# Sample rows in column halves, even column groups, another tile order, and inputs fetched a stage ahead, in a whole decoder layer on one core

## The reference

```
h = rmsnorm(x) * (1 + sc1) + sh1                 # sc, sh, gt from silu(c) @ ada_w
q, k, v, qi, ki, wi, hq, hf, hi, hg = split(h @ w_in)     # 3656 columns
score = sum_h wi[h] * relu(qi[h] . ki)           # 8 index heads x 64
keep the 256 best admissible keys of each query
a = rmsnorm(softmax(q . k over the kept keys) @ v)        # 8 heads, 4 kv heads, x 64
r = gated linear recurrence(hq, hf, hi) per head of 128   # state 128 x 128, 4 heads
r = rmsnorm(r) * silu(hg)
x = x + gt1 * (concat(a, r) @ w_out)
h = rmsnorm(x) * (1 + sc2) + sh2
x = x + gt2 * moe(h)                             # top 1 of 4 groups, top 2 of its 4 experts
y = rmsnorm(x) * (1 + scf) + shf
```

## Time and profile before

| | us |
|---|---|
| median of 3 runs | 1861.36 (1853.93 to 1866.20) |
| the profiled execution, its own time | 1853.43 |
| its span, first to last instruction | 1851.7 |
| TensorE busy | 1618.0 (87%) |
| VectorE busy | 840.5 (45%) |
| ScalarE busy | 388.0 (21%) |
| GpSimd busy | 205.6 (11%) |

### The profile page before, as it was taken

How to read it: one execution, slowest core, us unless ns; L and a number is a source line. 1 busy time by engine, 2 the same in 40 slices (tenths; PEclk the granted TensorE clock), 3 DMA queues, 4 the chain that set the end, 5 groups by cost and what they waited for, 6 DMA issues and landing times. The chain is left out here.

```text
span 1851.7 us, 20887 instructions
## 1 busy us (share of the span) xinstructions
PE 1618.0 (87%) x7594; PEld 784.4 (42%) x7595; DVE 840.5 (45%) x1935; ACT 388.0 (21%) x780; POOL 205.6 (11%) x176
## 2 busy tenths in 40 slices
PE   5998899999999979989996996961799999999970
PEld 3553334444443357765443752641233333333320
DVE  3123469999999135543215452756111111111116
ACT  4003442321111145432224341210000000000002
POOL 0001001100000000010022330100111111111112
PEclk9999999999999989999998798985899999999985
DMA  9112113332333240016447035624899999999924
GB/s 337 47 47 80 46 46 115 119 122 76 122 127 123 81 164 1 1 59 263 183 186 251 13 129 163 213 97 160 311 336 357 367 347 346 348 350 324 326 71 193
DMA packets 133098, 326.21 MB, mean 176 GB/s; under 512 B 16497, under 2 KB 23945, under 8 KB 130442
## 3 DMA queue, kind: packets, MB, share of 16 engines
q1 hardware_dynamic: 116826, 241.95, 37.1%
q0 software_dynamic: 16176, 82.98, 13.5%
HBM read 281.93 MB, written 42.97 MB: 175 GB/s over the span
## 5 line engine op out<-in xcount | busy, mean ns | idle before, releaser
L2639 PE MATMUL banks<-arena 128*64 x1008 | 438.6, 595 | 5.4 <-issue 2.6
L2640 PE MATMUL banks<-arena 128*64 128x512 f32 x1008 | 438.7, 595 | 0.0
L1175 PE MATMUL banks<-arena 128*128 128x512 f32 (+2 forms) x960 | 384.3, 557 | 0.3 <-ACT arena L1308 0.3
L1175 PEld LDWEIGHTS banks<-arena 128*128 128x128 f32 (+1 forms) x960 | 167.4, 188 | 220.7 <-issue 215.1
L2639 PEld LDWEIGHTS banks<-arena 128*64 128x64 f32 x1008 | 136.6, 137 | 282.2 <-issue 282.2
L1459 DVE TENSOR_SCALAR_CACHE_REDUCE arena<-arena 128x384 uint8<-128x384 f32 (+3 forms) x224 | 246.0, 1142 | 3.4
L2640 PEld LDWEIGHTS banks<-arena 128*64 128x64 f32 x1008 | 136.7, 137 | 0.0
L2708 DVE TENSOR_TENSOR arena<-arena,banks 128x256 f32<-128x256 f32 x42 | 15.8, 418 | 262.8 <-PE banks L2640 262.8
L2690 ACT ACTIVATE arena<-banks 128x512 f32<-128x512 f32 x21 | 12.5, 597 | 465.7 <-PE banks L2640 465.7
L1726 DVE CUSTOM_DVE_ANT_0 arena<-banks,arena 128x512 f32<-128x512 f32 (+3 forms) x96 | 51.4, 575 | 76.9 <-PE banks L1662 76.9
L2719 DVE SCALAR_TENSOR_TENSOR arena<-banks,arena 128x1024 f32<-128x1024 f32 x21 | 27.0, 1284 | 129.5 <-PE banks L2640 129.5
(11 more groups left out here) (415 smaller groups left out, 1986.0 us busy)
## 6 DMA issues: line engine op xcount, KB each, us to landing
arena<-in_w SPq DMA_DIRECT2D x63, 2048.0 KB, 13.0
arena<-in_ada_w SPq DMA_DIRECT2D x12, 2048.0 KB, 9.1
arena<-in_w_in SPq DMA_DIRECT2D x7, 2048.0 KB, 7.8
arena<-in_ada_final_w SPq DMA_DIRECT2D x4, 2048.0 KB, 8.1
arena<-in_x_prompt SPq DMA_DIRECT2D x4, 1024.0 KB, 8.2
tmp_hf<-arena SPq DMA_DIRECT2D x16, 256.0 KB, 2.0
tmp_hq<-arena SPq DMA_DIRECT2D x16, 256.0 KB, 2.0
arena<-in_x_prompt SPq DMA_DIRECT2D x8, 512.0 KB
```

The lines of the kernel that those rows point to most:

```text
L1175: ins = pe.matmul(ps[0:m, ring[n] % 2, 0:cols], lhs(a), rhs(a), start=(a == 0), stop=(a == KD - 1))
L2639: pe.matmul(ps[0:HP, bank, :], x[:, 0:HP], Wt[:, bass.ds(at, 1), off:off + width].rearrange("p o a -> p (o a)"), **kw)
L2640: return pe.matmul(ps[HP:P, bank, :], x[:, HP:P], Wt[:, u, off:off + width], **kw)
```

## The change

Five things change. (1) In `front` each product of the 64 sample rows is issued as two of 256 columns, whose results go to the lower and the upper 64 partitions of a bank; ScalarE copies two halves. (2) The feature chunks' column groups are 363, 363 and 362 wide. (3) `prompt_attention` takes tile 7 first and tile 0 last: `tile(n)` stands wherever n // 4 or i named a tile, and i only counts. (4) In `hgrn` the first eight partial rows have a place each in R, and the transposed attention goes to buffers that the norms use later; `scaled` waits for the stores instead. (5) The modulation rows, norm gains, router weights and x of tiles 0 and 1 are loaded in `hgrn`, behind SyncE's waits for the end of certain parts, into places that have come free; some buffers of `project_out` move.

```diff
+O_GT, O_SH, O_XR, O_G2 = O_HQ, O_S0, O_S0 + 2 * D, O_HF
+O_WR = O_G2 + D
...
+def next_inputs(k):
+    ar = k.ar
+    gt, sc, sh = ar.view(O_GT, 2, D), ar.view(O_GT + 2 * D, 2, D), ar.view(O_SH, 2, D)
+    return gt, sc, sh, ar.view(O_G2, D), [ar.view(O_XR + b * D, D) for b in range(2)], ar.view(O_WR, KD, NR)
...
@@ hgrn @@
     def turned_to(i):
-        return (R[:, i % 2, :] if i < NPRE else V[:, 4 + i % 2, :]).rearrange("p (a n) -> p a n", n=P)
+        return ((sq, sqa)[i % 2] if i < NPRE else V[:, 4 + i % 2, :]).rearrange("p (a n) -> p a n", n=P)
     def staged(n):
-        return R[:, 4 + n % 4, :] if n < 2 * NPRE else V[:, n % 4, :]
+        return R[:, 1 + n, :] if n < 2 * NPRE else V[:, n % 4, :]
...
@@ hgrn, sync @@
+            gt, sc, sh, g2, x, wr = next_inputs(k)
+            moves = scale_shift_parts(k, (g2, t["norm2_g"]), [(gt, 2), (sc, 4), (sh, 3)])
+            sp.wait_ge(s["att"], NQ)
+            sp.dma_start(*moves[6]).then_inc(k.s_next["mod"], 16)
+            sp.dma_start(wr[:, :, 0:4], t["w_group"].rearrange("o (a p) n -> p (o a) n", p=P)).then_inc(k.s_next["wr"], 16)
+            sp.dma_start(wr[:, :, 4:NR], t["w_expert_router"].rearrange("o (a p) n -> p (o a) n", p=P)).then_inc(k.s_next["wr"], 16)
             sp.wait_ge(s["sa"], 2 * GH)
-            sp.dma_start(t["hgrn_sample"].rearrange("o s h p e -> p (o s) h e"), S0.rearrange("p s (h e) -> p s h e", e=DK)).then_inc(s["out"], 16)
+            sp.dma_start(t["hgrn_sample"].rearrange("o s h p e -> p (o s) h e"), S0.rearrange("p s (h e) -> p s h e", e=DK)).then_inc(k.s_next["s0"], 16)
+            sp.wait_ge(s["o"], NQ)
+            for move in moves[0:4]:
+                sp.dma_start(*move).then_inc(k.s_next["mod"], 16)
+            sp.wait_ge(k.s_next["s0"], 16)
+            for move in moves[4:6]:
+                sp.dma_start(*move).then_inc(k.s_next["mod"], 16)
+            for b in range(2):
+                sp.dma_start(x[b], x_rows(t, b)).then_inc(k.s_next[f"x{b}"], 16)
             sp.wait_ge(s["st"], 4 * NCH)
             sp.dma_start(t["hgrn_prompt"].rearrange("a b h p e -> p (a b h) e"), S[NCH % RING]).then_inc(s["out"], 16)
             for n in range(2 * NPRE, 2 * NT):
                 store(n)
-            sp.wait_ge(s["out"], 32)
+            sp.wait_ge(s["out"], 16)
...
@@ hgrn, scalar: rows(n) and scaled(q) @@
-                if n >= 4:
+                if n >= 2 * NPRE:
                     act.wait_ge(k.s_part[n % 4], 16 * (n // 4))
-                if q >= 5:
-                    act.wait_ge(k.s_part[q - 5], 32)
+                if q != 1:
+                    act.wait_ge(k.s_part[(i - 1) % 4], 32)
...
@@ projection_groups @@
-                for c, n in ((0, 512), (512, 512), (1024, NS)):
+                for c, n in ((0, 363), (363, 363), (726, 362)):
...
@@ front, tensor (the same in first and project) @@
+                    if m == NS:
+                        for x in range(2):
+                            ins = pe.matmul(ps[x * NS:(x + 1) * NS, ring[n] % 2, 0:256], lhs(a), rhs(a)[:, x * 256:(x + 1) * 256], start=(a == 0), stop=(a == KD - 1))
+                    else:
+                        ins = pe.matmul(ps[0:m, ring[n] % 2, 0:cols], lhs(a), rhs(a), start=(a == 0), stop=(a == KD - 1))
...
@@ front, scalar (the same in first and for q, k, v) @@
+                if m == NS:
+                    act.activation(stage[n % 4][0:m, 0:256], ps[0:NS, bank, 0:256], func, scale=scale)
+                    act.activation(stage[n % 4][0:m, 256:512], ps[NS:P, bank, 0:256], func, scale=scale).then_inc(s["pev"], 1)
...
@@ prompt_attention @@
+    def tile(n):
+        return NT - 2 - n // 4
     def pieces(n):
-        return (n // 4 + 4) // 4
+        return (tile(n) + 4) // 4
     def width(n, c):
-        return min(512, P * (n // 4 + 1) - 512 * c)
+        return min(512, P * (tile(n) + 1) - 512 * c)
-            logits(0, 0)
-            logits(1, 0)
+            for n in range(2):
+                for c in range(pieces(n)):
+                    logits(n, c)
...
@@ project_out @@
+    gt, sc, sh, g2, x, wr = next_inputs(k)
+    o = O_V
     h2 = [ar.view(o + j * D, D) for j in range(2)]; o += 2 * D
...
             load_part(0)
-            sp.dma_start(x[0], x_rows(t, 0)).then_inc(s["x0"], 16)
-            sp.dma_start(x[1], x_rows(t, 1)).then_inc(s["x1"], 16)
-            load_scale_shift(sp, k, s["mod"], (g2, t["norm2_g"]), [(gt, 2), (sc, 4), (sh, 3)])
-            sp.dma_start(wr[:, :, 0:4], t["w_group"].rearrange("o (a p) n -> p (o a) n", p=P)).then_inc(s["wr"], 16)
-            sp.dma_start(wr[:, :, 4:NR], t["w_expert_router"].rearrange("o (a p) n -> p (o a) n", p=P)).then_inc(s["wr"], 16)
             load_part(1)
```

More of the change, by code:

```diff
@@ L130, in __init__ @@
         self.s_gates = nc.alloc_semaphore("gates")
+        self.s_next = {n: nc.alloc_semaphore("next_" + n) for n in ("mod", "x0", "x1", "wr", "s0")}
         self.s_wo = [nc.alloc_semaphore(f"w_out{b}") for b in range(3)]
@@ L1159, in first @@
                 for a in range(KD):
-                    ins = pe.matmul(ps[0:r, b, :], hT[:, a, i * P:i * P + r], wp[0][:, a, :], start=(a == 0), stop=(a == KD - 1))
+                    if r == NS:
+                        for v in range(2):
+                            ins = pe.matmul(ps[v * NS:(v + 1) * NS, b, 0:256], hT[:, a, i * P:i * P + r], wp[0][:, a, v * 256:(v + 1) * 256], start=(a == 0), stop=(a == KD - 1))
+                    else:
+                        ins = pe.matmul(ps[0:r, b, :], hT[:, a, i * P:i * P + r], wp[0][:, a, :], start=(a == 0), stop=(a == KD - 1))
                 ins.then_inc(s["m1"], 1)
@@ L1174, in project @@
                 for a in range(KD):
-                    ins = pe.matmul(ps[0:m, ring[n] % 2, 0:cols], lhs(a), rhs(a), start=(a == 0), stop=(a == KD - 1))
+                    if m == NS:
+                        for x in range(2):
+                            ins = pe.matmul(ps[x * NS:(x + 1) * NS, ring[n] % 2, 0:256], lhs(a), rhs(a)[:, x * 256:(x + 1) * 256], start=(a == 0), stop=(a == KD - 1))
+                    else:
+                        ins = pe.matmul(ps[0:m, ring[n] % 2, 0:cols], lhs(a), rhs(a), start=(a == 0), stop=(a == KD - 1))
                 ins.then_inc(s["pmm"], 1)
@@ L1649, in queries @@
                 for u in range(4):
-                    ins = pe.transpose(ps[:, 6 + i % 2, u * P:(u + 1) * P], z[:, i, QC + u * P:QC + (u + 1) * P], k.ident)
+                    ins = pe.transpose(ps[:, 6 + i % 2, u * P:(u + 1) * P], z[:, tile(4 * i), QC + u * P:QC + (u + 1) * P], k.ident)
                 ins.then_inc(s["tr"], 1)
@@ L1685, in weigh @@
                     ins = pe.matmul(ps[:, 6 + i % 2, h * HD:(h + 1) * HD], PT[q % 4][:, v, :], z[:, u, VC + (h // 2) * HD:VC + (h // 2 + 1) * HD],
-                                    start=(u == 0), stop=(u == i))
+                                    start=(u == 0), stop=(u == tile(n)))
                 ins.then_inc(s["pv"], 1)
@@ L1747, in _ @@
                 ve.tensor_copy(kT[:, :, i * P:(i + 1) * P], ps[:, i % 4, 0:2 * P].rearrange("p (h n) -> p h n", n=P)).then_inc(s["kc"], 1)
-            masked(0, 0)
-            masked(1, 0)
+            for n in range(2):
+                for c in range(pieces(n)):
+                    masked(n, c)
             for n in range(NU):
@@ L1767, in powers @@
             def powers(n):
-                N, at = P * (n // 4 + 1), pieces(n) - 1
+                N = P * (tile(n) + 1)
                 for x in range(2):
```

28 lines of the change are left out of this document (17 added, 11 removed).

## The result

The changed kernel takes 1798.25 us (median of 4 runs, 1797.21 to 1799.05), the kernel before 1857.78 beside it (4 runs): a ratio of 0.967, 95% interval 0.9635 to 0.9712. Two further sets of runs of the same changed kernel gave 1799.25 and 1797.51 us (0.9652, interval 0.9618 to 0.9686; 0.9650, 0.9619 to 0.9681). The kernel before, run beside those two sets, had medians of 1862.23 and 1865.35 us, so by medians the change brought 59.5, 63.0 and 67.8 us. The forecast of 1813 us had the sign, and 1798 lies at the lower end of its range (1797 to 1836): the kernel is some 15 us faster than forecast.

The account below looks back on a forecast made before the run. TensorE, busy most of the span, was taken as the bound, through its work and its gaps. Terms 17.0 + 7 + 2 + 9 + 13.5 - 4 = 44.5 us off 1853.43 gave 1808.9, with half of 7.9 carried over 1813; range 1797 to 1836.

Parts of the forecast that it names:

- Column halves: In `front`, five sample-row products as two alternating 256-column halves save 3.40 us a group, 17.0 us; ends 16 and 17.
- The rival in which the halves neither overlap nor load under each other: In `front`, a sample group takes 11.3 us, so 21 us are lost instead of 17 won: 1851 us; chance 0.03.
- 363 columns: In `front`'s feature chunks, groups of 363 columns cost near their proportion of a 512 group: 7 us gained, ends 0 and 7.7.
- the rival of a slow stream: In `front`, 363-column instructions run slowly as odd streams; at double price the kernel takes 1932 us; chance 0.05.
- Tile order: In prompt attention, largest tiles first avoids slow-clock work at the start: 2 us gained; ends a gain of 5, a loss of 8.
- The rival that the sparse end hands a slow clock to the sample attention: The slow spell stretches over prompt attention's sparse end into sample attention, 10 us worse than forecast: 1823; chance 0.15.
- Own places: Ahead of the recurrence, eight row places end ScalarE's store wait: 9 us gained after giving back 1; ends 5 and 10.
- Next stage's inputs: At `project_out`'s start, inputs loaded during the recurrence end VectorE's and TensorE's wait: 13.5 us gained; ends 9 and 15.
- SyncE's price: Behind the recurrence, loads ahead of row stores delay row copy 12 and TensorE's last tile: 4 us lost, from 0 to 8.
- The rival in which both together win nothing: Row stores stall the recurrence's last tiles for all that the inputs save in `project_out`: 1822; chance 0.12.

Follow-up runs that it names:

- e1_whole: Changed kernel with the sample tile's five groups in `front` whole again, 16 instructions over 512 columns each; 1818.35 us, 19.1 more.
- e6_seq: Changed kernel with the sample groups' column halves in `front` issued one after the other instead of in turn; 1815.33 us, 16.1 more.
- e2_512: Changed kernel with the feature groups cut in 512, 512 and 64 columns again; 1811.70 us, 12.5 more.
- e5_late: Changed kernel with x, modulation rows, gains and router weights loaded at the start of `project_out` again; 1815.30 us, 17.8 more.
- e4_ring: Changed kernel with the partial rows ahead of the recurrence in four places again, each waiting for an earlier store; 1812.02 us, 14.5 more.

## Why the prediction was right, and where its sizes were off

**The sum holds without the clock.** With the estimated lost clock taken off, the kernel before stands at 1802.6 us and the three profiles of the changed one at 1757.4 in the mean: 45 less, where the terms made 44.5. That they agree so well is in part luck: the gain by the inputs and the price for SyncE were both put too high, by 1.4 to 3.9 and by 2.5 to 3.4 us, and the one is subtracted from the other. The forecast missed by 15 us in two steps. It carried over half of the 7.9 us by which the first median of before lay above its profile; the changed kernel's median lies 0.6 above its profile, so most of the 4 us were not there. And it gave the clock a place in one term only, while about 10 us less were lost over all stages: 4.3 less in prompt attention, 5.1 in the recurrence, 1.9 ahead of it, 2.4 in `project_out`, 0.6 in `front`, against 2.6 more in sample attention and 1.7 in the rest (first profile of the changed kernel).

**Column halves**, 17.0: 17.1 by the rows, 18.5 by e1_whole. The sample attention's line L1946 was the right row to price it by, and it has what e6_seq shows to matter: its halves take turns. The rival in which the halves neither overlap nor load under each other falls with the 3.60 us; its price of 11.3 us a group appears nowhere, not in e6_seq either (6.25). By an estimate, two thirds of the factor of 2.38 that the Trainium skill ("TensorE: Matmul & The Clock Gate", section "Measured speedup vs the span model") gives for three column tiles would have made the term 13. The trace has 7.01 / 3.60 = 1.95 for two.

**363 columns**, 7: 6.6 by the rows, 8.5 by e2_512. An instruction takes 4.99 / 16 = 0.312 us, near the proportion, and the rival of a slow stream falls.

**Tile order**, 2: the stage is 6.4 us shorter, 2.1 of it with the clock taken off. The step that failed is how the clock was counted: the forecast took one slow spell at one place, 2.5 to 5 us, as a property of the order, and the gain came out beyond the term's good end of 5. With the same order the stage lost 3.1 us in the six profiles whose instructions up to there are the same, and 3.4, 5.8 and 10.8 where `front` differs (e1, e6, e2). So the mechanism behind this term, that the order sets the clock, is not shown. The rival that the sparse end hands a slow clock to the sample attention asked for 10 us; 2.6 more were lost there, and e1 and e5 lose only 0.9 to 1.1 more with the same order.

**Own places**, 9: the stretch is 10.5 us shorter, 8.5 with the clock taken off, 9.0 to 9.2 by e4_ring. The 1 us that the forecast gave back for GpSimd's products beside VectorE's was not paid: VectorE's key products are now done before GpSimd starts. The recurrence's 5.7 us were in no term; 5.1 of them are lost clock.

**Next stage's inputs**, 13.5: 12.1 us, 9.6 with the clock taken off; 11.2 to 12.8 by e5_late. The mechanism is the one named; the size was 1.4 too large, as the forecast counted the new start at full clock and its first 10 us ran at 0.50 and 0.89 (3.1 us lost, before 1.7). The 9.6 is a lower bound, for some of the lost clock goes with the wait: behind it TensorE ran at 0.50 for 5 us before (1146.42 to 1151.42) and in e5_late (1104.43 to 1109.43), and none of the eleven profiles without the wait has a slow spell at that place. **SyncE's price**, 4: the wait is there with 7.22 us, but TensorE felt 1.39 of it, and the part is 0.6 to 1.5 us longer. The step that was off is that ScalarE's wait was counted as TensorE's. The rival in which both together win nothing falls.

So the mechanisms stand as put, but for the clock in the tile order. Sum the medians of the five undone parts, though, and 19.1 + 12.5 + 9.0 + 14.5 + 17.8 = 73 us come out for a change that brought 63.0 and 67.8 us in the sets beside them; less lost clock it is 20 + 8 + 4 + 10 + 7 = 49 for 45. A part of the difference is that the changed kernel's profiles lose little in two stages (3.1 and 4.9 us in prompt attention and recurrence, no run here has less), and that most edits to it, a shift of 2 us too, come out with more lost there. Each edit has one profile, so how much of that the edit brings is open.

## What to carry to other kernels

Where rows fill half of the array's output side, issue the two column halves in turn, instruction by instruction; one after the other they win little (0.76 us a group here, not 3.41). Price an edit at full clock and set the lost clock of each stage beside it: it moved by 3 to 8 us here in stages that the edit doesn't touch, so an undo run's total says less than its own stage. A clock that fell in a wait was part of that wait's price here, though, and one that was low ahead of a wait cost nothing. Loads moved into an earlier stage delayed the stores behind them, in SyncE's order of issue and in the queue; the waits on those stores cost only what TensorE's spare bank didn't cover (1.39 of 7.22 us).

## What the runs showed that was not expected

TensorE's instructions for the two halves can run ahead of each other: in e6_seq the products of L1191 for the lower half started at 124.66, 0.21 us before one that stands ahead of them in the order for the upper half (124.87). The Trainium skill ("TensorE: Matmul & The Clock Gate", section "The mechanism") says that products start and end strictly in their order; these rows differ for products on different halves, as far as the profile's starts can be trusted at 0.2 us.

And the same TensorE instructions of the recurrence took 60.1, 61.6 and 63.2 us, with one slow spell of three lengths; what sets its length is open.
